# One trunk kernel: the convolution kept in fp32, VectorE making the gated products, GpSimd normalising the first token half

## The chip, the cores and the metric

The kernel runs on one core of one Trainium2 chip. The metric is the time of one execution in microseconds (us), the median of three runs.

## The reference

Two layers over 256 tokens of width 2048, all in fp32. Layer 0 mixes tokens with a gated linear recurrence, layer 1 with causal attention; each mixer is followed by a squared-ReLU MLP (2048 to 8192 and back), and each of the four sub-layers ends in `x = LayerNorm(alpha*x + sublayer(x))`. The recurrence, which the change touches:

```
gate, u = split(x @ w_in)
u = causal depthwise convolution of width 4 (u) + conv_b
r = sigmoid(u_blocks @ gate_a_w + b);  i = sigmoid(u_blocks @ gate_x_w + b)
log_a = -8 * r * softplus(-lam);       a = exp(log_a)
b = u * i * sqrt(-expm1(2*log_a))
h = associative_scan over tokens of (a, b):  h_t = a_t*h_{t-1} + b_t
y = (gelu(gate) * h) @ w_out
```

LayerNorm: mean and variance over the 2048 columns of a token, `(x-mean)*rsqrt(var+eps)*g + b`.

## The kernel before

Every large product is made of three products of fp32r operands: both factors are split into a high part (a copy rounded to fp32r) and a low part (the difference), and high*high, low*high and high*low are added in PSUM. Activations are split once; weights are split as they stream. A *turn* is 512 output columns over all 2048 inputs; its weights come in 8 *blocks* of 128x1024. For each block SyncE issues a 512 KB load into one of 8 staging buffers (`wst`, L230), ScalarE copies the high part (`split_hi`, L638), VectorE subtracts the low part (`split_lo`, L860), and TensorE multiplies. There are 4 buffers each for high and low parts, so a split may start when TensorE has finished the block four before (`mm_done`), and a load may start when the split eight before is done (`wl_done`). The order on each engine is written out by hand: `splits(b, lo, hi)` issues the splits of positions lo to hi-1 relative to the turn at block b, and the other work of the engine stands between such calls. Position 8 and above belong to the next turn's blocks. The lists `work` (L729 for ScalarE, L989 for VectorE) say after how many splits of a turn which step comes.

The recurrent mixer has four U turns (the input of the convolution), four short gate groups (L466) whose sigmoids give r (`r3`) and i (`i3`), four G turns (the gate branch), then the out projection. During the U turns the convolution of each group of 4 channel chunks is made in the scratch tile `e1` (ScalarE begins it, L662; VectorE adds three taps, L918), and its high and low parts go to `hid`, which TensorE reads for the gate groups. During the G turns GpSimd adds the two parts again into `e1`, multiplies `i3` by it (L339 to L347), and later by the root (L349 to L354); ScalarE makes the decays and roots (L704, L712), VectorE the last step of the root (L963), the scans (L969) and the product with the gate (L976). The tile `acc` (the same memory as `gate`) takes the output of the G turns, group by group (L740).

At the end of each sub-layer stands `last_pair` on TensorE (L519) and ScalarE (L746) and `last_turn` on VectorE (L1043). The last turn finishes token half 0 before half 1, so half 0's statistics are made while TensorE works on half 1. Half 0 is normalised by VectorE (column groups 0 and 1) and ScalarE (groups 2 and 3, L757), half 1 by VectorE after `add_half(1)` (L1051). TensorE then transposes the normalised tokens in eight pairs of chunks (`norm_pair`, L504), ScalarE applies gain and bias (L771), VectorE splits the result (L1071), and the next sub-layer's first turn starts. While TensorE waits it issues small dummy products (`keep_warm`, L448). The rows of gain and bias for the residual are loaded by SyncE (`load_rows`, L278) at points of its queue between the weight loads; `load_rows(2)` stands ahead of the second MLP's weights and waits for `prepped`, which VectorE raises in `prepare` (L1011).

Of the kernel before, what the change touches and what calls it, by code (L numbers as in the profile page):

```python
# [29 lines left out]
P = 128  # L30
T = 256
# [49 lines left out]
Z_DVE = 2 + NG  # L81
# [5 lines left out]
def build_trunk(nc, x, ln_g, ln_b, mlp_w1, mlp_w2, rg_w_in, rg_conv_w, rg_conv_b, rg_gate_a_w,  # L87
                rg_gate_a_b, rg_gate_x_w, rg_gate_x_b, rg_lambda, rg_w_out, moba_w_qkv, moba_w_out,
                rope, out):
    with ExitStack() as ctx:  # L90
# [27 lines left out]
        tok = sb("tok", [P, 3, HALVES])  # L118
# [22 lines left out]
        std, rstd, shift = tok[:, 0, :], tok[:, 1, :], tok[:, 2, :]  # L141
# [24 lines left out]
        ui_sum = sem("ui_sum")  # L166
# [21 lines left out]
        ln_shift = sem("ln_shift")  # L188
        z_dve = sem("z_dve")
        z_act = sem("z_act")  # L190
# [34 lines left out]
        def _(sp):  # L225
# [86 lines left out]
            load_rows(2)  # L312
# [11 lines left out]
        def _(pool):  # L324
# [13 lines left out]
            pool.wait_ge(sig_done, 4)  # L338
            for g in range(NG):  # L339
                rows = slice(g * GROUP, (g + 1) * GROUP)  # L340
                if g >= 1:
                    pool.wait_ge(ui_ready, g)
                pool.tensor_tensor(e1[:, :, :], hid[:, rows, 0, :], hid[:, rows, 1, :], ALU.add)\
                    .then_inc(ui_sum, 1)
                pool.wait_ge(ui_sum, g + 1)
                pool.tensor_tensor(i3[:, rows, :], i3[:, rows, :], e1[:, :, :], ALU.mult)\
                    .then_inc(ui_ready, 1)  # L347

            for g in range(NG):  # L349
                rows = slice(g * GROUP, (g + 1) * GROUP)  # L350
                pool.wait_ge(rec_link, g + 1)
                pool.wait_ge(ui_ready, g + 1)
                pool.tensor_tensor(i3[:, rows, :], i3[:, rows, :], r3[:, rows, :], ALU.mult)\
                    .then_inc(b_ready, 1)  # L354
# [3 lines left out]
        def _(pe):  # L358
# [145 lines left out]
            def norm_pair(n, k):  # L504

                g = 2 * k // GROUP
                pe.wait_ge(z_dve, Z_DVE * n + g + 3)
                if g >= 2:
                    pe.wait_ge(z_act, 2 * n + g - 1)
# [9 lines left out]
            def last_pair(b, ready, free, n):  # L519
# [14 lines left out]
                keep_warm(6)  # L534
# [96 lines left out]
        def _(act):  # L631
# [25 lines left out]
            def conv_hi_part(g):  # L657
                act.wait_ge(conv_link, (g + 1) * (CONV - 1))
                act.activation(hid[:, g * GROUP:(g + 1) * GROUP, 0, :], e1[:, :, :], ACT.Copy)\
                   .then_inc(conv_hi, 1)  # L660

            def conv_start(g):  # L662

                act.wait_ge(psum_free, T_U + g + 1)
                if g >= 1:
                    act.wait_ge(pair_ready, R_CONV + 2 * g)
                for c in range(g * GROUP, (g + 1) * GROUP):
                    tap = C_CONVW + (CONV - 1) * NC + c
                    ins = act.activation(e1[:, c % GROUP, :], u3[:, c, :], ACT.Identity,
# [52 lines left out]
            def product_hi(g):  # L722
# [6 lines left out]
            work = (((2, decay, 0), (2, decay, 1)), ((2, decay, 2), (2, decay, 3)),  # L729
                    ((1, root, 0), (0, root, 1), (1, root, 2), (1, root, 3), (2, gelu, 0), (0, gelu, 1)),  # L730
                    ((0, product_hi, 0), (2, product_hi, 1), (2, gelu, 2), (0, product_hi, 2)))
            for t in range(NG):
# [6 lines left out]
                splits(b, no, off, LATE)  # L739
                take_hl(t % 2, b, acc[:, t * GROUP:(t + 1) * GROUP, :], hl_copied)  # L740
# [5 lines left out]
            def last_pair(b, no, n):  # L746
# [3 lines left out]
                splits(b, no, START, BLOCKS)  # L750
                act.wait_ge(ln_var, 2 * n + 1)
                act.activation(std[:, 0:1], mv[:, 0, 1:2], ACT.Sqrt, bias=eps[:, 0:1]).then_inc(ln_root, 1)
                if n < 3:
                    splits(b, no, BLOCKS, BLOCKS + 1)
                    act.wait_ge(ln_inv, 2 * n + 1)
                    act.wait_ge(ln_shift, n + 1)
                    for g in (2, 3):  # L757
                        cols = slice(g * COLS, (g + 1) * COLS)
                        act.activation(res[:, 0, cols], res[:, 0, cols], ACT.Identity, scale=rstd[:, 0:1],
                                       bias=shift[:, 0:1]).then_inc(z_act, 1)  # L760
                        if g == 2:
                            splits(b, no, BLOCKS + 1, BLOCKS + 2)
# [92 lines left out]
        def _(dve):  # L855
# [187 lines left out]
            def last_turn(b, free, n):  # L1043
# [62 lines left out]
                for g0 in range(2):  # L1106
                    z(0, g0)
# [167 lines left out]
```

## Time and profile before

| | us |
|---|---|
| median of three runs | 2162.43 (2161.63 to 2163.31) |
| the profiled execution | 2167.35 |
| its span, first to last instruction | 2165.4 |
| TensorE busy | 2130.8 |
| VectorE busy | 1322.9 |
| ScalarE busy | 977.2 |
| GpSimd busy | 40.4 |

The page names engines PE (TensorE matmul), PEld (its weight load), DVE (VectorE), ACT (ScalarE), POOL (GpSimd) and SP (SyncE). Busy times overlap between engines. A trailing bracket in a row is the idle time of the engine ahead of it and what ended it.

### The profile page before, as it was taken

How to read it: one execution, taken by the hardware profiler on the slowest of the kernel's cores; microseconds unless marked ns; L12 is line 12 of the kernel's file. 1: busy time of each engine (PE TensorE's matmuls, PEld its weight loads, DVE VectorE, ACT ScalarE, POOL GpSimd, SP SyncE). 2: the span in 40 equal slices, each digit the busy share in tenths (PEclk: the TensorE clock that was granted, in tenths of full speed). 3: DMA queues.
4: the chain of work that ended last, by engine and by line, in shares of the span. 5: the costliest groups of instructions: out<-in, count | busy, mean ns of one | idle time of the engine just before them, and what ended most of it. 6: DMA issues, size and time to landing. Idle time of an engine off the chain costs nothing.

```text
span 2165.4 us, 31017 instructions
## 1 busy us (share of the span) xinstructions
PE 2130.8 (98%) x10966; PEld 1815.2 (84%) x10966; DVE 1322.9 (61%) x1241; ACT 977.2 (45%) x1091; POOL 40.4 (2%) x22
## 2 busy tenths in 40 slices
PE   9998999999999999999999999999999999999997
PEld 8887878888888888888888888878888888888886
DVE  6788766555554655555767566665655555555556
ACT  5585545434443443443544445344434434434442
POOL 0042000000000000000000000000000000000000
PEclk9999999999999999999999999999999999999999
DMA  8555765666666566656454546556666666566663
GB/s 275 186 167 163 243 195 175 193 195 189 187 190 192 179 198 193 185 186 194 138 177 161 185 156 218 180 189 190 194 194 186 188 192 190 175 201 186 191 190 134
DMA packets 210481, 406.14 MB, mean 188 GB/s; under 512 B 12480, under 2 KB 18880, under 8 KB 209376
## 3 DMA queue, kind: packets, MB, share of 16 engines
q1 hardware_dynamic: 210400, 405.00, 59.7%
q8 instruction: 58, 0.95, 0.2%
q14 instruction: 23, 0.19, 0.0%
HBM read 402.85 MB, written 2.10 MB: 187 GB/s over the span
## 4 chain that ended last, share of the span: by engine, by line
PE 94%; DVE 3%; issue 1%; ACT 1%; DMA 1%; SPq 0%; DVEq 0%; ACTq 0%
PE ps L383 39%; PE ps L373 32%; PE ps L374 16%; PE ps L607 1%; PE ps L605 1%; PE ps L606 1%; DVE wl L860 1%; PE ps L452 1%; PE ps L515 1%; DVE f L972 1%; ACT wh L638 0%; PE ps L620 0%; PE ps L486 0%; PE ps L487 0%; PE ps L485 0%
## 5 line engine op out<-in xcount | busy, mean ns | idle before, releaser
L860 DVE TENSOR_TENSOR wl<-wst,wh 128x1024 fp32r<-128x1024 f32 x744 | 924.1, 1251 | 666.4 <-ACT wh L638 664.4
L638 ACT ACTIVATE wh<-wst 128x1024 fp32r<-128x1024 f32 x744 | 782.9, 1059 | 905.2 <-PE ps L383 468.5
L373 PE MATMUL ps<-xin,wh 128*128 128x512 f32 x3072 | 1090.7, 400 | 7.4 <-DVE wl L860 7.4
L374 PE MATMUL ps<-xin,wl 128*128 128x256 f32 x3072 | 862.9, 281 | 0.0
L373 PEld LDWEIGHTS ps<-xin,wh 128*128 128x128 f32 x3072 | 578.4, 188 | 151.9 <-DVE wl L860 9.7
L383 PE MATMUL ps<-wh,hid 128*128 128x512 f32 x2560 | 694.9, 389 | 0.0
L374 PEld LDWEIGHTS ps<-xin,wl 128*128 128x128 f32 x3072 | 581.3, 189 | 0.2
L383 PEld LDWEIGHTS ps<-wh,hid 128*128 128x128 f32 x2560 | 479.9, 188 | 99.5
L383 PE MATMUL ps<-wl,hid 128*128 128x512 f32 x1280 | 404.4, 389 | 0.0
L383 PEld LDWEIGHTS ps<-wl,hid 128*128 128x128 f32 x1280 | 240.3, 188 | 49.9
L870 DVE TENSOR_TENSOR e<-e,ps 128x1024 f32<-128x1024 f32 x32 | 39.1, 1221 | 50.2 <-ACT e L647 50.2
L796 ACT ACTIVATE hid<-e 128x1024 f32 x32 | 34.0, 1062 | 54.6 <-DVE e L1141 54.6
L647 ACT ACTIVATE e<-ps 128x1024 f32<-128x1024 f32 x32 | 32.8, 1026 | 56.5 <-PE ps L374 56.5
L1034 DVE TENSOR_TENSOR f<-f,ps 128x1024 f32<-128x1024 f32 (+1 forms) x36 | 44.0, 1222 | 16.5 <-PE ps L383 16.5
L605 PE MATMUL ps<-wh,xin 128*128 128x512 f32 x128 | 50.7, 396 | 0.0
L607 PE MATMUL ps<-wl,xin 128*128 128x512 f32 x128 | 49.9, 390 | 0.0
L606 PE MATMUL ps<-wh,xin 128*128 128x512 f32 x128 | 49.8, 389 | 0.0
L1145 DVE TENSOR_TENSOR hid<-e,hid 128x1024 f32 x32 | 39.2, 1226 | 10.4 <-ACT hid L796 10.4
L1141 DVE SCALAR_TENSOR_TENSOR e<-e 128x1024 f32<-128x1024 f32 x32 | 39.2, 1225 | 1.1
L771 ACT ACTIVATE f<-ps,prm 128x256 f32<-128x256 f32 x48 | 24.2, 567 | 19.6 <-PE ps L515 19.6
L452 PE MATMUL ps<-ones 128*128 128x128 f32 x100 | 18.4, 350 | 12.7 <-DVE f L1051 10.5
L452 PEld LDWEIGHTS ps<-ones 128*128 128x128 f32 x100 | 16.7, 256 | 14.1 <-DVE f L1051 11.8
(116 smaller groups left out, 692.5 us busy)
## 6 DMA issues: line engine op xcount, KB each, us to landing
wst<-in_mlp_w_dram SPq DMA_DIRECT2D x512, 512.0 KB, 3.8
wst<-in_moba_w_qkv_dram SPq DMA_DIRECT2D x96, 512.0 KB, 4.1
wst<-in_rg_w_in_dram SPq DMA_DIRECT2D x64, 512.0 KB, 4.3
wst<-in_rg_w_out_dram SPq DMA_DIRECT2D x32, 512.0 KB, 3.9
wst<-in_moba_w_out_dram SPq DMA_DIRECT2D x32, 512.0 KB, 4.7
gate<-in_ln_g_dram SPq DMA_DIRECT2D x4, 1024.0 KB, 7.0
gate<-in_ln_b_dram SPq DMA_DIRECT2D x4, 1024.0 KB, 9.0
f<-in_x_dram SPq DMA_DIRECT2D x8, 256.0 KB, 7.9
```

What stands on the lines that cost most here:

```text
L373: pe.matmul(dst[:, n, :], wh[:, s, w], src[:, c, :, :], start=(c == 0), stop=False)
L374: mm = pe.matmul(dst[:, n, 0:T], wl[:, s, w], src[:, c, 0, :], start=False, stop=(c == NC - 1))
L383: return pe.matmul(banks(half)[:, a, :], hid[:, c, part, a * P:(a + 1) * P], (wl if low else wh)[:, s, w], start=(c == 0 and part + low == 0),
L452: pe.matmul(ps[:, warm_bank, 0:P], ones[:, :], ones[:, :], start=True, stop=True)
L605: pe.matmul(X[:, a, :], xin[:, c, 0, tok], wh[:, s, w], start=(c == 0), stop=False)
L606: pe.matmul(X[:, a, :], xin[:, c, 1, tok], wh[:, s, w], start=False, stop=False)
L607: mm = pe.matmul(X[:, a, :], xin[:, c, 0, tok], wl[:, s, w], start=False, stop=(c == NC - 1))
L638: act.activation(wh[:, off % SPLITS, :], wst[:, kb, :], ACT.Copy).then_inc(wh_done, 1)
L860: dve.tensor_tensor(wl[:, off % SPLITS, :], wst[:, off % BLOCKS, :], wh[:, off % SPLITS, :], ALU.subtract).then_inc(wl_done, 1)
L1034: dve.tensor_tensor(res[:, :, cols], res[:, :, cols], banks(half)[:, 0:HALVES, :], ALU.add)\
L1141: dve.scalar_tensor_tensor(out=e2[:, :, :], in0=e1[:, :, :], scalar=0.0, in1=e1[:, :, :], op0=ALU.max, op1=ALU.mult).then_inc(sq_val, 1)
L1145: dve.tensor_tensor(hid[:, rows, 1, :], e2[:, :, :], hid[:, rows, 0, :], ALU.subtract)\
```

## The change

In the mixer the convolution is accumulated in `acc` instead of `e1` and stays there in fp32 until the G turn of the same group overwrites it. GpSimd's sum of the two parts goes. The product `i3 * u` (`gated_input`) is made by VectorE in the first G turn and the product with the root by VectorE right behind the root step in the second G turn; ScalarE's roots are in the second turn instead of the third, its decays three in the first turn and one in the second. ScalarE's copy out of PSUM into `acc` waits for `ui_ready`. Scans, gelus and products have other places in the lists.

At the first three norms GpSimd normalises all of token half 0; ScalarE makes three weight copies in its place; VectorE takes the reciprocal ahead of its two splits. `keep_warm(6)` becomes `keep_warm(3)`. The third load of gain and bias rows is issued by ScalarE in the third `last_pair` instead of by SyncE.

```diff
@@ -309,7 +306,6 @@
                 load_turn(moba_w_out[0], t * COLS, B_MO + t * BLOCKS)
-            load_rows(2)
             load_mlp(1, B_MLP1)
@@ -335,23 +331,12 @@
-            pool.wait_ge(sig_done, 4)
-            for g in range(NG):
-                rows = slice(g * GROUP, (g + 1) * GROUP)
-                if g >= 1:
-                    pool.wait_ge(ui_ready, g)
-                pool.tensor_tensor(e1[:, :, :], hid[:, rows, 0, :], hid[:, rows, 1, :], ALU.add)\
-                    .then_inc(ui_sum, 1)
-                pool.wait_ge(ui_sum, g + 1)
-                pool.tensor_tensor(i3[:, rows, :], i3[:, rows, :], e1[:, :, :], ALU.mult)\
-                    .then_inc(ui_ready, 1)
-
-            for g in range(NG):
-                rows = slice(g * GROUP, (g + 1) * GROUP)
-                pool.wait_ge(rec_link, g + 1)
-                pool.wait_ge(ui_ready, g + 1)
-                pool.tensor_tensor(i3[:, rows, :], i3[:, rows, :], r3[:, rows, :], ALU.mult)\
-                    .then_inc(b_ready, 1)
+            for n in range(3):
+                for g in range(NG):
+                    cols = slice(g * COLS, (g + 1) * COLS)
+                    pool.wait_ge(ln_inv, 2 * n + 1)
+                    pool.tensor_scalar(res[:, 0, cols], res[:, 0, cols], mv[:, 0, 0:1], rstd[:, 0:1],
+                                       ALU.subtract, ALU.mult).then_inc(z_pool, 1)
@@ -504,9 +489,8 @@
                 g = 2 * k // GROUP
-                pe.wait_ge(z_dve, Z_DVE * n + g + 3)
-                if g >= 2:
-                    pe.wait_ge(z_act, 2 * n + g - 1)
+                pe.wait_ge(z_pool, NG * n + g + 1)
+                pe.wait_ge(z_dve, NG * n + g + 1)
                 if k >= 4:
@@ -531,7 +515,7 @@
                     norm_pair(n, k)
-                keep_warm(6)
+                keep_warm(3)
@@ -656,17 +640,15 @@
                 act.wait_ge(conv_link, (g + 1) * (CONV - 1))
-                act.activation(hid[:, g * GROUP:(g + 1) * GROUP, 0, :], e1[:, :, :], ACT.Copy)\
-                   .then_inc(conv_hi, 1)
+                rows = slice(g * GROUP, (g + 1) * GROUP)
+                act.activation(hid[:, rows, 0, :], acc[:, rows, :], ACT.Copy).then_inc(conv_hi, 1)
...
                 act.wait_ge(psum_free, T_U + g + 1)
-                if g >= 1:
-                    act.wait_ge(pair_ready, R_CONV + 2 * g)
                 for c in range(g * GROUP, (g + 1) * GROUP):
                     tap = C_CONVW + (CONV - 1) * NC + c
-                    ins = act.activation(e1[:, c % GROUP, :], u3[:, c, :], ACT.Identity,
+                    ins = act.activation(acc[:, c, :], u3[:, c, :], ACT.Identity,
                                          scale=prm[:, tap:tap + 1], bias=prm[:, C_CONVB + c:C_CONVB + c + 1])
@@ -726,9 +708,10 @@
-            work = (((2, decay, 0), (2, decay, 1)), ((2, decay, 2), (2, decay, 3)),
-                    ((1, root, 0), (0, root, 1), (1, root, 2), (1, root, 3), (2, gelu, 0), (0, gelu, 1)),
-                    ((0, product_hi, 0), (2, product_hi, 1), (2, gelu, 2), (0, product_hi, 2)))
+            work = (((1, decay, 0), (2, decay, 1), (2, decay, 2)),
+                    ((1, decay, 3), (2, root, 0), (0, root, 1), (1, root, 2), (1, root, 3)),
+                    ((6, gelu, 0), (0, gelu, 1)),
+                    ((1, product_hi, 0), (1, product_hi, 1), (1, gelu, 2), (1, product_hi, 2)))
             for t in range(NG):
@@ -737,6 +720,7 @@
                 splits(b, no, off, LATE)
+                act.wait_ge(ui_ready, t + 1)
                 take_hl(t % 2, b, acc[:, t * GROUP:(t + 1) * GROUP, :], hl_copied)
@@ -748,18 +732,14 @@
                 splits(b, no, START, BLOCKS)
+                if n == 2:
+                    act.wait_ge(prepped, NG * (n + 1))
+                    for dst, src in ((gain_row, ln_g), (bias_row, ln_b)):
+                        act.dma_start(dst, src[1, 0:1, :].to_broadcast([P, D])).then_inc(rows_loaded, 16)
                 act.wait_ge(ln_var, 2 * n + 1)
...
                 if n < 3:
-                    splits(b, no, BLOCKS, BLOCKS + 1)
-                    act.wait_ge(ln_inv, 2 * n + 1)
-                    act.wait_ge(ln_shift, n + 1)
-                    for g in (2, 3):
-                        cols = slice(g * COLS, (g + 1) * COLS)
-                        act.activation(res[:, 0, cols], res[:, 0, cols], ACT.Identity, scale=rstd[:, 0:1],
-                                       bias=shift[:, 0:1]).then_inc(z_act, 1)
-                        if g == 2:
-                            splits(b, no, BLOCKS + 1, BLOCKS + 2)
+                    splits(b, no, BLOCKS, BLOCKS + 3)
                 act.wait_ge(ln_var, 2 * n + 2)
@@ -772,8 +752,8 @@
                     ins.then_inc(v_done, 1)
-                    if k in (1, 2, 3, 4):
-                        off = BLOCKS + 1 + k
+                    if k in (1, 2, 3):
+                        off = BLOCKS + 2 + k
                         splits(b, no, off, off + 1)
@@ -960,11 +940,19 @@
+            def gated_input(g):
+                rows = slice(g * GROUP, (g + 1) * GROUP)
+                dve.wait_ge(sig_done, 2 * (g // 2) + 2)
+                dve.tensor_tensor(i3[:, rows, :], i3[:, rows, :], acc[:, rows, :], ALU.mult).then_inc(ui_ready, 1)
+
             def root(g):
...
                                          in1=r3[:, rows, :], op0=ALU.add, op1=ALU.mult).then_inc(rec_link, 1)
+                dve.wait_ge(ui_ready, g + 1)
+                dve.wait_ge(rec_link, g + 1)
+                dve.tensor_tensor(i3[:, rows, :], i3[:, rows, :], r3[:, rows, :], ALU.mult).then_inc(b_ready, 1)
@@ -986,10 +974,11 @@
-            work = ((), (),
-                    ((1, root, 0), (0, root, 1), (1, root, 2), (0, root, 3), (1, states, 0), (1, states, 1)),
-                    ((0, product, 0), (0, product_lo, 0), (1, states, 2), (0, product, 1), (1, product_lo, 1),
-                     (1, states, 3), (0, product, 2), (1, product_lo, 2)))
+            work = (((1, gated_input, 0), (1, gated_input, 1), (1, gated_input, 2), (1, gated_input, 3)),
+                    ((3, root, 0), (1, root, 1), (1, root, 2), (1, root, 3)),
+                    ((1, states, 0), (1, states, 1), (2, states, 2), (2, states, 3)),
+                    ((0, product, 0), (1, product_lo, 0), (0, product, 1), (1, product_lo, 1),
+                     (2, product, 2), (1, product_lo, 2)))
             for t in range(NG):
@@ -1064,8 +1053,8 @@
-                def z(h, g):
-                    dve.tensor_scalar(res[:, h, cols_for(g)], res[:, h, cols_for(g)], mv[:, h, 0:1], rstd[:, h:h + 1],
+                def z(g):
+                    dve.tensor_scalar(res[:, 1, cols_for(g)], res[:, 1, cols_for(g)], mv[:, 1, 0:1], rstd[:, 1:2],
                                       ALU.subtract, ALU.mult).then_inc(z_dve, 1)
@@ -1099,17 +1088,12 @@
                     return
-                splits(b, BLOCKS, BLOCKS + 1)
                 inverse(0)
-                dve.scalar_tensor_tensor(out=shift[:, 0:1], in0=mv[:, 0, 0:1], scalar=-1.0, in1=rstd[:, 0:1],
-                                         op0=ALU.mult, op1=ALU.mult).then_inc(ln_shift, 1)
-                for g0 in range(2):
-                    z(0, g0)
-                splits(b, BLOCKS + 1, BLOCKS + 2)
+                splits(b, BLOCKS, BLOCKS + 2)
                 add_half(1)
...
                 for g0 in range(NG):
-                    z(1, g0)
+                    z(g0)
                 for k in range(STEPS):
```

Left out: the removed semaphores and the third row of `tok`, and the convolution's lines in which `e1` becomes `acc`.

## Rows read from the trace of the kernel before

**Rows 1.** The page's busy times: engine, us, share of the span, instructions.

```profile
PE 2130.8 (98%) x10966; PEld 1815.2 (84%) x10966; DVE 1322.9 (61%) x1241; ACT 977.2 (45%) x1091; POOL 40.4 (2%) x22
```

**Rows 2.** TensorE's waits: line, releaser, us in total, times, longest us.

```profile
PE ps L452 <- DVE f L1051: 10.5, 3, 4.8
PE ps L373 <- DVE wl L860: 7.4, 7, 3.3
```

**Rows 3.** Windows: the four G turns, then four turns of an MLP; columns as printed.

```profile
core 0: us, PE busy (x) PEld busy (x) DVE busy (x) ACT busy (x) POOL busy (x), PEclk, DMA share, GB/s
126.15:226.28 100.13, 92.72 (x516) 79.12 (x515) 86.35 (x61) 64.50 (x88) 38.58 (x12) 0.98 0.51 162
502.80:593.20 90.40, 90.40 (x513) 78.37 (x513) 50.56 (x42) 39.43 (x38) 0.00 (x0) 1.00 0.61 187
```

**Rows 4.** Timeline of GpSimd in the G turns: start, us, engine, line, operation.

```profile
138.76 3.27 POOL L346 TENSOR_TENSOR f<-f,e 128x1024 f32<-128x1024 f32 x1
...
181.11 6.69 POOL L353 TENSOR_TENSOR f<-f 128x1024 f32<-128x1024 f32 x2 [25.69 <-DVE f L966]
```

**Rows 5.** Timeline of VectorE in the G turns.

```profile
130.49 26.01 DVE L860 TENSOR_TENSOR wl<-wst,wh 128x1024 fp32r<-128x1024 f32 x8 [3.40 <-ACT wh L638]
...
211.59 2.43 DVE L972 TENSOR_TENSOR_SCAN f<-f 128x256 f32<-128x256 f32 x4
```

**Rows 6.** Timeline of ScalarE in the G turns.

```profile
134.56 1.71 ACT L707 ACTIVATE f<-f,small 128x256 f32<-128x256 f32 x4
136.17 1.69 ACT L709 ACTIVATE f<-f,small 128x256 f32<-128x256 f32 x4
...
178.71 2.01 ACT L714 ACTIVATE f<-f 128x1024 f32<-128x1024 f32 x2
```

**Rows 7.** Timeline of the first norm, ScalarE, VectorE and TensorE.

```profile
309.89 0.29 ACT L752 ACTIVATE tok<-mv,eps 128x1 f32<-128x1 f32 x1 [6.07 <-DVE mv L1060]
...
310.09 1.05 ACT L638 ACTIVATE wh<-wst 128x1024 fp32r<-128x1024 f32 x1
...
311.17 1.22 DVE L860 TENSOR_TENSOR wl<-wst,wh 128x1024 fp32r<-128x1024 f32 x1 [1.31 <-ACT wh L638]
...
313.15 0.39 PE L383 MATMUL ps<-wl,hid 128*128 128x512 f32 x1
...
314.55 1.23 DVE L860 TENSOR_TENSOR wl<-wst,wh 128x1024 fp32r<-128x1024 f32 x1 [0.97 <-ACT wh L638]
...
315.69 0.68 DVE L1051 TENSOR_TENSOR f<-f,ps 128x512 f32<-128x512 f32 x1
...
316.42 2.83 PE L452 MATMUL ps<-ones 128*128 128x128 f32 x16 [2.88 <-DVE f L1051]
...
321.66 0.69 DVE L1076 TENSOR_TENSOR xin<-f,xin 128x512 fp32r<-128x512 f32 x1
...
322.07 1.50 PE L452 MATMUL ps<-ones 128*128 128x128 f32 x12
...
323.33 0.47 PE L373 MATMUL ps<-xin,wh 128*128 128x512 f32 x1
```

**Rows 8.** GpSimd's masks at L333: min/median/max ns, first and last start, forms.

```profile
L333 POOL TENSOR_SCALAR_AFFINE_SELECT maskt<-maskt x2: 295/352/408, 1.9 to 2.2; 128x128 f32<-128x128 f32 x1, 128x256 f32<-128x256 f32 x1
```

**Rows 9.** Timeline of the second norm, VectorE and TensorE.

```profile
1043.86 0.69 DVE L1076 TENSOR_TENSOR xin<-f,xin 128x512 fp32r<-128x512 f32 x1
...
1044.71 0.48 PE L373 MATMUL ps<-xin,wh 128*128 128x512 f32 x1
```

**Rows 10.** Timeline of the third norm, SyncE, ScalarE and TensorE.

```profile
1419.82 0.35 SPq L285 DMA_DIRECT2D gate<-in_ln_g_dram  x1
...
1421.32 38.12 SPq L230 DMA_DIRECT2D wst<-in_mlp_w_dram  x16
...
1428.52 1.06 ACT L638 ACTIVATE wh<-wst 128x1024 fp32r<-128x1024 f32 x1 [1.77 <-DMA wst<-in_mlp_w_dram]
...
1434.87 3.44 PE L452 MATMUL ps<-ones 128*128 128x128 f32 x16 [4.76 <-DVE f L1051]
```

More of the change, by code:

```diff
@@ L80 @@
 HELD = BLOCKS - SPLITS
-Z_DVE = 2 + NG
 C_LNG, C_LNB, C_CONVW, C_CONVB, C_BA, C_BX, C_LAM = 0, 64, 128, 192, 208, 224, 240
@@ L117, in build_trunk @@
         mv = sb("mv", [P, HALVES, 2])
-        tok = sb("tok", [P, 3, HALVES])
+        tok = sb("tok", [P, 2, HALVES])
         stat = sb("stat", [P, 4, 8])
@@ L140, in build_trunk @@
         norm_t = f3[:, :].rearrange("p (c t) -> p c t", t=T)
-        std, rstd, shift = tok[:, 0, :], tok[:, 1, :], tok[:, 2, :]
+        std, rstd = tok[:, 0, :], tok[:, 1, :]
         stage_full = [sem(f"stage_full{s}") for s in range(BLOCKS)]
@@ L165, in build_trunk @@
         sig_done = sem("sig_done")
-        ui_sum = sem("ui_sum")
         b_ready = sem("b_ready")
@@ L187, in build_trunk @@
         ln_inv = sem("ln_inv")
-        ln_shift = sem("ln_shift")
         z_dve = sem("z_dve")
-        z_act = sem("z_act")
+        z_pool = sem("z_pool")
         v_done = sem("v_done")
@@ L926, in conv_step @@
                     col = C_CONVW + (CONV - 1 - k) * NC + c
-                    ins = dve.scalar_tensor_tensor(out=e1[:, q, k:T], in0=u3[:, c, 0:T - k],
-                                                   scalar=prm[:, col:col + 1], in1=e1[:, q, k:T],
+                    ins = dve.scalar_tensor_tensor(out=acc[:, c, k:T], in0=u3[:, c, 0:T - k],
+                                                   scalar=prm[:, col:col + 1], in1=acc[:, c, k:T],
                                                    op0=ALU.mult, op1=ALU.add)
@@ L934, in conv_lo @@
                 dve.wait_ge(conv_hi, g + 1)
-                dve.tensor_tensor(hid[:, rows, 1, :], e1[:, :, :], hid[:, rows, 0, :], ALU.subtract)\
+                dve.tensor_tensor(hid[:, rows, 1, :], acc[:, rows, :], hid[:, rows, 0, :], ALU.subtract)\
                    .then_inc(pair_ready, 2)
```

## The prediction

> **What bounds the kernel now.** I read the page's busy table first: TensorE is busy 2130.8 us, 98% of the span, so only its idle stretches and its slow stretches can be won [rows 1]. The waits of TensorE say which idle stretches an engine causes: 10.5 us in three pieces behind the addition of the last sub-layer half (L1051), 7.4 us in seven pieces behind VectorE's low parts of the weights (L860) [rows 2]. Everything else of its idle time is the start and the output's tail, which the change leaves alone. Then I compared two stretches of equal work. Four turns of the gate projection take 100.13 us, four turns of the same shape inside an MLP 90.40 us with TensorE busy throughout [rows 3]. So the recurrent mixer loses 9.7 us in those four turns; the 7.4 us of waits are part of it, the rest is restarts and a granted clock of 0.98 instead of 1.00 in the same rows.
>
> Why it loses them stands in the next two groups. GpSimd runs twelve 128x1024 operations there, 3.3 us each beside VectorE [rows 4]. While it does so, eight splits of VectorE take 26.01 us, 3.25 us each [rows 5], where one alone takes 1.22 us [rows 7] (the line at 311.17). TensorE eats a block of weights in 90.40/32 = 2.83 us, so VectorE falls behind by 0.4 us a block, and by much more once the roots are added.
>
> The Trainium skill (SBUF — State Buffer, Who interferes with whom) gives the rule behind this: a VectorE instruction with two SBUF inputs and a GpSimd instruction that reads SBUF exclude one another for the whole instruction, not by halves. The trace agrees: 3.3 us is about one GpSimd operation plus one of VectorE.
>
> **Mixer, part by part.** GpSimd's twelve operations go, so VectorE's 32 splits cost 1.22 us each. VectorE gets eight new operations instead (four products u*i in the first gate turn, four with the root in the second), 128x1024 with two inputs like a split, 1.22 each, 9.8 us. Is that hidden? VectorE's work of the four turns is then 32 splits, 4 additions of the high halves, 4 root steps, 3 products and 3 low parts inside the turns and the 8 new ones, 54 x 1.22 = 65.9 us, and 16 scans at 2.43 us for four [rows 5], 9.7 us: 75.6 of 90.4 us. It fits on average; what counts is the worst place. A split may begin when TensorE ends the block four before, and is wanted three blocks later: 3 x 2.83 = 8.5 us, less the copy on ScalarE (1.05) and the split (1.22), leaves 6.2 us of debt that VectorE may run up. In the second gate turn four root pairs stand between splits: 3 x 1.22 = 3.66 us per split against 2.83, a debt of 0.83 x 4 = 3.3 us. Then come two splits and the addition, 3.66 us against 5.66, and the third turn has six splits and four groups of scans, 7.3 + 9.7 = 17.0 us against 17.0. Deepest debt about 4 us, so some 2 us remain and TensorE does not stop.
>
> ScalarE: in the first gate turn it has three decays (3.3 us each without the table load [rows 6]) between splits: 3.3 + 1.3 (load) + 1.05 = 5.7 us against 2.83, debt 2.8, paid back by the next two splits. Its eight splits, three decays, the load and the copy out of PSUM are about 20.7 of 22.6 us. In the second turn one decay, four roots of 1.0 us, a load: 18 us. The new wait ahead of the copy out of PSUM (for the product u*i of that group) has the turn's last split queued behind it; the product is ready some 10 us before, as it is VectorE's third operation. The convolution's accumulator moves to another tile with the same shapes: nothing. Its start no longer waits for the low part before it, but no TensorE wait stands in that stage: nothing. So the term is -9.7 us; bounds -10 and, if VectorE's debt overruns, -5.
>
> **Three norms.** The chain now, in the first [rows 7]: root of half 0 done at 310.18, ScalarE's split at 310.09, VectorE's at 311.17; reciprocal and two normalisations; ScalarE's next copy only at 313.5 (314.55 less its 1.05), between two normalisations; VectorE's split at 314.55; the addition of half 1 at 315.69. TensorE ended at 313.15 + 0.39 = 313.54, so this addition is 2.1 us late, which is the 2.88 us that TensorE stands. After the change ScalarE copies three blocks in a row and VectorE takes the reciprocal (0.16 us) first, then the two splits, whose copies end at 310.09 + 1.05 = 311.14 and at 312.2. Alone they would end at 313.5 and the whole 2.1 us would be won. But GpSimd starts its four 128x512 normalisations at 310.5, and two of them come in ahead of the two splits. Let p be the price of one: the addition falls at 310.5 + 2p + 2 x 1.15 + small change = 312.8 + 2p, or 313.6 if that is later; gain = 315.69 - that = 2.9 - 2p.
>
> p isn't in the trace. Nearest rows: a one-input GpSimd operation on 256 columns took 0.41 us [rows 8], the lower end; a two-input one on 1024 columns takes up to 3.4 us beside VectorE [rows 4], of which 1.2 us is VectorE's turn, so 2.2 us: the upper end, unlikely for a quarter of the operands. I take twice the first, 0.8 us, since it is one input and twice the columns. Gain 1.3 us a norm, 3.9 in all; bounds 2.1 (6.3) and -1.5 (-4.5). The addition itself has one input in PSUM.
>
> The Trainium skill (GPSIMD Engine Reference, Engine selection and its section on performance) says that a one-input operation there runs roughly at line rate and only a two-input one is held back. By that p would be near 0.5 us and the gain near 1.9 us a norm; no row here shows it.
>
> What is late next is the chain from the addition to the first product of the next turn, 315.69 to 323.33 [rows 7]. Its dummy products shrink from 12 records (322.07 to 323.33, 1.26 us) to 6: 0.63 us less. The data that the next turn waits for is there at 321.66 + 0.69 = 322.35, so all 0.63 are won. In the second norm the data comes at 1044.55 and TensorE begins at 1044.71 [rows 9]: only 0.1. The third is like the second. Together -0.8 us. GpSimd's groups 3 and 4 are wanted only inside the next turn.
>
> **Third norm.** SyncE waits there until 1419.82 to load the gain and bias rows, and only then issues the MLP's weights; the first lands so late that ScalarE stands 1.77 us, TensorE 4.76 instead of 2.88 us [rows 10]. The two row loads go to ScalarE, behind its seventh and eighth splits; the wait for the preparation is over by then (VectorE's last step is what released SyncE at 1419.82), ScalarE has nothing until the root that ends at 1428.52 - 1.77 = 1426.75, and behind the wait only the root is queued. The weights go out as buffers come free, 20 us earlier. Term: -(4.76 - 2.88) = -1.9 us.
>
> **Sum.** -9.7 - 3.9 - 0.8 - 1.9 = -16.3 us. The profiled execution took 2167.35 us (span 2165.4 plus 1.95), so it would take 2151.0. The runs shown have a median of 2162.43, 4.9 less; on them it is 2146.1. I say 2146.0.
>
> **Rivals.** (a) TensorE keeps its high clock in the norms. After 2.88 us of standing (4.76 in the third) it falls to its lower level, 1.2 of 2.4 GHz: sixteen dummy records take 2.83 us [rows 7] and 3.44 us [rows 10], against 16 x 0.105 = 1.7 us at the rate of the later twelve. Stalls of 0.3 us did not do this, 1.6 us is not in the trace. If it holds, the chain of 7 us shortens until VectorE and ScalarE carry it, by about 1.0 us a norm: 2143. For: the stand is nearly halved. Against: the dummy products are light, and the slow stretch covers them.
> (b) GpSimd is slow and the splits wait for it. p = 2.2: gain -1.5 instead of 1.3, 8.4 us more in all: 2154.5. For: the lock of rows 5. Against: one input, half the columns.
> (c) VectorE becomes the bound of the gate turns: waits for ScalarE's roots add to the debt, TensorE stands about 1 us per root or scan group, 4 to 5 us, with the clock's fall: 2151. For: 2 us of reserve are small. Against: the average of 75.6 in 90.4.
> (d) Slower than before, by one mechanism: GpSimd's normalisations ahead of the two splits, so long that they eat the mixer's gain too. The norms must then lose 9.7 + 0.8 + 1.9 = 12.4 us, 4.1 each: 2.9 - 2p = -4.1, p = 3.5 us. At p = 4 it is 2165.4. No row has anything that long for 512 columns.
> (e) The new order does not do what it says, because GpSimd's part is wanted before it is there (first group by 318.4): needs p over 2.5, so it goes with (b) and (d).
>
> **How the numbers follow.** Forecast 0.55 (2144 to 2149), (a) 0.2, (b) 0.1, (c) 0.12, (d) 0.03. The range must take in (a) with p at its lower end (2143 - 2.4 = 2140.6) and (c); most of (b) may stay out on the slow side: 2140.5 to 2153. What can be told from no change is 0.2%, 4.3 us. Faster 0.96, same 0.02 (between (b) and (d)), slower 0.02.
>
> **What would show it.** The four gate turns at 90 to 91 us with no TensorE wait on L860, and no split over 1.3 us there. The clock's dip at 0.98 of that stretch gone. In each norm TensorE standing about 1.6 us instead of 2.88, in all three alike; two splits of about 1.9 us, GpSimd's operations next to them about 0.8 us, or 2 us with the wait for VectorE. ScalarE's split of the third norm not waiting for a transfer. The forecast is wrong if the gate turns take over 93 us, if the addition of half 1 still comes 2 us after TensorE's last product, or if the dummy products run at full rate.

## The result, and the profile after

| | before | after |
|---|---|---|
| median, us | 2162.87 (4 runs) | 2142.89 (4 runs) |
| profiled execution, us | 2167.35 | 2144.91 |
| span, us | 2165.4 | 2143.1 |
| GpSimd busy, us | 40.4 | 29.8 |

The ratio is 0.9903, 95% interval 0.9891 to 0.9914: the change takes 20 us off, where 16.3 were forecast (2146.0, range 2140.5 to 2153). The time lies in the range; the mixer came out as forecast, the norms gave more than their terms. It lies outside the 2144 to 2149 that the forecast itself allowed, and on the 2143 of rival (a).

The gate turns of the profile after, beside four turns of an MLP in the same trace; this answers to [rows 3].

```profile
124.61:215.06 90.45, 90.45 (x515) 78.47 (x514) 72.10 (x70) 64.95 (x88) 0.00 (x0) 1.00 0.64 198
480.70:571.10 90.40, 90.40 (x504) 78.14 (x503) 50.54 (x42) 39.72 (x39) 0.00 (x0) 1.00 0.63 187
```

From the last gate product's start (124.48) to the out projection's first product (215.06) it is 90.6 us, 100.1 before. The mixer's turns now take what any turns of that shape take, TensorE is never idle in them and the granted clock stays at 1.00 (2.4 GHz). VectorE is less busy than before (72.1 against 86.35 us) although it does eight operations more (the window catches one split more as well). TensorE's waits answer to [rows 2]: the wait on the weights' low parts (L860 before, L840 now) is gone, and the 10.5 us behind the addition of half 1 (L1051, now L1040) are 2.3:

```profile
PE ps L437 <- DVE f L1040: 2.3, 3, 0.8
```

The first norm after the change, the timelines of ScalarE, VectorE, GpSimd and TensorE, answering to [rows 7].

```profile
298.87 2.00 ACT L622 ACTIVATE wh<-wst 128x1024 fp32r<-128x1024 f32 x2
...
298.99 0.17 DVE L1053 RECIPROCAL tok<-tok 128x1 f32<-128x1 f32 x1 [0.36 <-ACT tok L740]
300.00 2.36 DVE L840 TENSOR_TENSOR wl<-wst,wh 128x1024 fp32r<-128x1024 f32 x2 [0.84 <-ACT wh L622]
302.36 0.69 DVE L1040 TENSOR_TENSOR f<-f,ps 128x512 f32<-128x512 f32 x1
...
304.63 2.92 DVE L1057 TENSOR_SCALAR f<-f,mv,tok 128x512 f32<-128x512 f32 x4
307.47 0.41 DVE L1063 CAST xin<-f 128x512 fp32r<-128x512 f32 x1
307.92 0.69 DVE L1065 TENSOR_TENSOR xin<-f,xin 128x512 fp32r<-128x512 f32 x1
...
299.26 9.32 POOL L338 TENSOR_SCALAR f<-f,mv,tok 128x512 f32<-128x512 f32 x4 [296.69 <-DVE tok L1053]
...
301.93 0.39 PE L368 MATMUL ps<-wl,hid 128*128 128x512 f32 x1
303.10 2.41 PE L437 MATMUL ps<-ones 128*128 128x128 f32 x16 [0.78 <-DVE f L1040]
...
307.25 0.83 PE L437 MATMUL ps<-ones 128*128 128x128 f32 x6
308.71 0.47 PE L358 MATMUL ps<-xin,wh 128*128 128x512 f32 x1 [0.63 <-issue]
```

Three readings. VectorE's two splits take 1.2 us each although GpSimd works beside them throughout; the addition comes at 302.36, as soon as TensorE's last product is through (301.93 + 0.39 = 302.32). GpSimd takes 9.32 us for four operations, 2.3 us each, just above the 2.2 that was the upper end. And VectorE's four normalisations take 2.92 us, 1.92 before the change. I call the time from TensorE's last product to the first of the next turn the norm's gap. The stand is the part of it in which TensorE waits ahead of its first dummy product. The gap was 9.8, 9.4 and 11.0 us in the three norms and is 6.4, 6.3 and 6.4: 11.1 us less. The stand was 2.88, 2.88 and 4.76 us and is 0.78 in all three, and the granted clock is 1.00 in all three gaps. With 9.6 of the mixer that makes 20.7 of the 22.4 us between the two profiled executions; the other 1.7 us lie before the gate groups (last of them at 126.15 and 124.48), in a part that the change does not speed up. The first product starts at 8.10 us instead of 8.88, since the input arrived earlier in this execution, and the first products run at full rate at once, where before they took 0.63 instead of 0.40 us until about 11 us. The medians do not depend on that one start, and their difference is 20.0.

### The profile page after: what moved, and what is told of

It is laid out like the page before. It is cut to its first block, busy times and chain, and to the rows that moved or that the text cites. A ratio compares the mean times of both kernels' runs of the same rounds, so it can differ in the third digit from the quotient of the medians.

```text
span 2143.1 us, 30984 instructions
## 1 busy us (share of the span) xinstructions
PE 2122.6 (99%) x10948; PEld 1807.5 (84%) x10948; DVE 1306.1 (61%) x1240; ACT 973.7 (45%) x1085; POOL 29.8 (1%) x22
## 4 chain that ended last, share of the span: by engine, by line
PE 97%; DVE 1%; issue 1%; ACT 0%; DMA 0%; SPq 0%; DVEq 0%; ACTq 0%
PE ps L368 40%; PE ps L358 34%; PE ps L359 17%; PE ps L591 1%; PE ps L589 1%; PE ps L590 1%; PE ps L499 0%; PE ps L604 0%; PE ps L472 0%; PE ps L471 0%; PE ps L470 0%; PE ps L579 0%; DVE bnst L1047 0%; DVE f L1040 0%; DMA f<-in_x_dram 0%
## 5 line engine op out<-in xcount | busy, mean ns | idle before, releaser
L840 DVE TENSOR_TENSOR wl<-wst,wh 128x1024 fp32r<-128x1024 f32 x744 | 903.1, 1223 | 665.2 <-ACT wh L622 663.2
L338 POOL TENSOR_SCALAR f<-f,mv,tok 128x512 f32<-128x512 f32 x12 | 28.0, 2342 | 1388.2 <-DVE tok L1053 1388.2
L591 PEld LDWEIGHTS ps<-wl,xin 128*128 128x128 f32 x128 | 24.0, 188 | 5.1
```

The source lines that it names most:

```text
L591: mm = pe.matmul(X[:, a, :], xin[:, c, 0, tok], wl[:, s, w], start=False, stop=(c == NC - 1))
L840: dve.tensor_tensor(wl[:, off % SPLITS, :], wst[:, off % BLOCKS, :], wh[:, off % SPLITS, :], ALU.subtract).then_inc(wl_done, 1)
```

## The experiments

The gaps below are read as in the last paragraph, the gate turns as in the rows above. e3 to e7, e9, e11 and e12 are one execution each: from them only stretches inside the trace are read.

**One part at a time.** e1: the kernel before with the mixer's hunks alone.

> The kernel before with the mixer's part alone (convolution in fp32, products on VectorE, roots and scans at their new places); norms as before. Theory: the four gate turns fall from 100.1 to 90.4 us, the rest is unchanged, so the time falls by 9.7 us (0.45%), ratio 0.9955, and the three norms still stand 2.9, 2.9 and 4.8 us with the clock falling to 1.2 GHz in each. Rival: part of the norms' gain of the full change comes from the shifted place in time, then the chains from the addition of half 1 to the next turn's first product get shorter than 7.6, 7.3 and 7.0 us here too, and the time falls by more than 11 us.

Ratio 0.9944 (0.9927 to 0.9961), median 2152.25 against 2164.31.

```profile
126.10:216.60 90.50, 90.50 (x515) 78.46 (x514) 72.11 (x70) 64.95 (x88) 0.00 (x0) 1.00 0.64 198
...
PE ps L436 <- DVE f L1044: 10.3, 3, 4.6
```

The gate turns are those of the full change, the stands of the norms those of before. The gaps are 9.8, 9.7 and 12.4 us: not shorter, the second and third even longer than before. So no gain of the norms comes from the mixer. The time fell by 12.1 us, more than the 11 of the rival, but not for the rival's reason: the traces have 9.6 us in the gate turns, 1.6 us lost in the gaps, and 4.0 us less between the norms (711.96 to 710.52 and 385.4 to 382.9), in stretches that the edit does not touch. The forecast ratio, 0.9955, lies in the interval.

The third gap is long because the clock stayed down longer. The six us behind the stand, in e1 and then in the kernel before, columns as in [rows 3]:

```profile
1421.30:1427.30 6.00, 6.00 (x28) 6.00 (x29) 3.28 (x8) 1.62 (x4) 0.00 (x0) 0.50 0.88 323
1434.90:1440.90 6.00, 6.00 (x41) 6.00 (x42) 4.01 (x9) 2.40 (x6) 0.00 (x0) 0.76 0.89 327
```

Behind the stand this norm took 7.8 us in e1 and 6.3 before, with the same instructions. What a fallen clock costs is therefore not one number.

e2: the norms' hunks and the row loads alone.

> The kernel before with the norms' part and the moved row loads alone; GpSimd keeps its twelve products in the mixer. Theory: the mixer still takes 100.1 us for its gate turns, the norms give what they gave in the full change (3.4 + 3.1 + 4.7 = 11.1 us), ratio 0.9949; the clock stays at 2.4 GHz in the norms and falls once, in the mixer. Rival (shifted place in time): the clock falls in one or more norms although the stand is 0.8 us; each costs about 1 us, and the gain is 8 to 10 us.

Ratio 0.9944 (0.9928 to 0.9961), gate turns 100.1 us, gaps 6.4, 6.3 and 6.4, and the clock falls once, in the mixer (0.98 there, 1.00 in all three gaps). The rival falls. Its TensorE waits:

```profile
PE ps L377 <- DVE wl L859: 6.5, 8, 3.3
PE ps L456 <- DVE f L1050: 2.3, 3, 0.8
```

The product of the two ratios is 0.9888; the full change measured again (e10, below) has 0.9903 with an interval of 0.9888 to 0.9918. The times could not show a loss by overlap of under about 0.3%. In the traces the full change has the gate turns of e1 (90.6 us) and the gaps of e2, so in the stretches that were changed nothing is lost.

**The lock, and GpSimd's price.** By the lock I mean that a two-input operation of VectorE and an operation of GpSimd wait for one another. e3 adds GpSimd work on a scratch tile in the gate turns (its waits and semaphores are left out here):

```diff
+            for i in range(6):
+                pool.tensor_scalar(e1[:, 0:2, :], e1[:, 0:2, :], eps[:, 0:1], ones[:, 0:1], ALU.subtract, ALU.mult)
+            for i in range(6):
+                pool.tensor_scalar(e1[:, 0:2, :], e1[:, 0:2, :], 0.5, 1.0, ALU.subtract, ALU.mult)
+            for i in range(4):
+                pool.tensor_tensor(e1[:, 0:2, :], e1[:, 0:2, :], e2[:, 0:2, :], ALU.mult)
+            for i in range(4):
+                pool.tensor_tensor(e1[:, :, :], e1[:, :, :], e2[:, :, :], ALU.mult)
```

> The full change with GpSimd work added during the gate turns on a scratch tile, whose values nothing reads: six tensor_scalar on 128x512 with scalars from memory (the form of the norms), six with constants, four tensor_tensor on 128x512, four on 128x1024. Theory: the tensor_scalar does not lock VectorE's two-input operations out: splits beside it stay at 1.22 us, as in the norms, and it takes 2.3 us itself; beside tensor_tensor a split takes 2.2 us (512 columns) and 3.3 us (1024). Rival: every GpSimd operation that reads SBUF locks, and in the norms the splits only happened to fall between: then some splits beside tensor_scalar take 2 us and more. On the duration: if the scalars' place in memory makes it slow, constants take about 0.8 us; if the two operations a column do, constants take 2.3 us as well.

GpSimd's four kinds (min/median/max ns, first and last start), then VectorE's timeline beside them.

```profile
L342 POOL TENSOR_SCALAR e<-e,eps,ones x6: 2076/3962/4997, 130.2 to 148.0; 128x512 f32<-128x512 f32 x6
L347 POOL TENSOR_SCALAR e<-e x6: 1924/1927/2957, 152.1 to 163.0; 128x512 f32<-128x512 f32 x6
L352 POOL TENSOR_TENSOR e<-e x4: 1982/2154/2165, 166.1 to 172.6; 128x512 f32<-128x512 f32 x4
L357 POOL TENSOR_TENSOR e<-e x4: 3204/3226/3243, 174.8 to 184.8; 128x1024 f32<-128x1024 f32 x4
```

```profile
139.85 1.21 DVE L868 TENSOR_TENSOR wl<-wst,wh 128x1024 fp32r<-128x1024 f32 x1
140.99 1.63 DVE L974 TENSOR_TENSOR f<-f,gate 128x1024 f32<-128x1024 f32 x1
142.67 1.22 DVE L868 TENSOR_TENSOR wl<-wst,wh 128x1024 fp32r<-128x1024 f32 x1
143.81 1.22 DVE L974 TENSOR_TENSOR f<-f,gate 128x1024 f32<-128x1024 f32 x1
...
171.31 2.31 DVE L979 SCALAR_TENSOR_TENSOR f<-f 128x1024 f32<-128x1024 f32 x1
...
179.07 3.39 DVE L979 SCALAR_TENSOR_TENSOR f<-f 128x1024 f32<-128x1024 f32 x1
```

Beside tensor_scalar VectorE's two-input operations take 1.2 us, now and then 0.2 to 0.4 more; it is GpSimd that is stretched, up to 5.0 us. Where its operation with scalars from memory began with VectorE idle it took 2.08 us, also when a split ran beside it afterwards. Beside tensor_tensor VectorE takes 2.3 us (512 columns) and 3.4 us (1024). So who pays hangs on GpSimd's kind of operation, and the kind that was moved into the norms is the one that lets VectorE's two-input operations through. Constants instead of scalars from memory save only 0.15 us of 2.08: it is the operation, with its two steps a column, that costs about 1.9 us for 512 columns. A tensor_scalar with one step was not run, so whether the steps or the kind make it slow is open.

e4 puts the old GpSimd load back, twelve tensor_tensor of 128x1024 at the old places on a scratch tile, with VectorE's products kept:

> The full change with twelve GpSimd tensor_tensor of 128x1024 added at the old places (eight from the last sigmoid on, four behind the root steps) on a scratch tile, whose values nothing reads. Theory: the lock alone made the old mixer slow; VectorE, which now has its own products besides, falls behind by more than before: the eight splits and four products beside the first eight take 3.3 us each, TensorE stands, and the gate turns take 100 us or more instead of 90.4. Rival: what slowed the old mixer was the place of the roots and scans in the third and fourth turns; then the gate turns stay under 95 us.

The four gate turns of e4, columns as in [rows 3]:

```profile
125.60:234.80 109.20, 97.33 (x515) 82.98 (x514) 96.60 (x70) 64.81 (x88) 34.68 (x12) 0.94 0.50 159
```

109.2 us instead of 90.5. With roots and scans at their new places GpSimd's traffic brings the old loss back, and more than it, since VectorE now has its own products besides. The rival falls. Beside the first eight operations stood five splits and three products of VectorE, nearly all at 3.4 us, not the twelve of the theory. The old places of roots and scans without GpSimd's operations were not run.

In the second gate turn of e4 a product of VectorE starts right behind one of GpSimd:

```profile
173.69 2.40 POOL L345 TENSOR_TENSOR e<-e 128x1024 f32<-128x1024 f32 x1 [19.12 <-DVE f L966]
173.72 3.46 DVE L970 TENSOR_TENSOR f<-f 128x1024 f32<-128x1024 f32 x1
```

VectorE waits out the whole of GpSimd's 2.40 us. A tensor_tensor of 1024 columns took 2.38 to 2.40 us all five times that it began first (four in e4, one in the kernel before), so the 3.2 us of e3 hold its wait for VectorE: under this kind both engines pay. Per column tensor_scalar is then the slower of the two on GpSimd, 1.9 us for 512 columns against an estimated 1.2 (half of 2.40).

**The parts of the norm.** e5: the third row load back on SyncE.

> The full change with the third load of the gain and bias rows back on SyncE ahead of the second MLP's weights. Theory: only the third norm changes; ScalarE's first copy there waits for a transfer again, until about 8.7 us after VectorE's last preparation step, and the addition of half 1 comes some 3 us later; TensorE's time from its last product to the first of the next turn goes from 6.4 to about 10 us with the clock falling to 1.2 GHz; the other two stay at 6.4 and 6.3. Rival: the transfer's delay only showed because of ScalarE's normalisations before; then the third norm stays within 1 us of 6.4.

The timeline of ScalarE in the third norm of e5:

```profile
1408.49 1.06 ACT L623 ACTIVATE wh<-wst 128x1024 fp32r<-128x1024 f32 x1 [1.78 <-DMA wst<-in_mlp_w_dram]
```

The wait of 1.77 us of [rows 10] is back, and the third gap is 8.2 us instead of 6.4, the others unchanged. The load was worth 1.8 us. My expectation of 10 us was too much: the addition came 2.0 and not 3 us later (stand 0.78 to 2.74), and that stand did not bring the clock down.

e7: six dummy products behind the transposes instead of three.

> The full change with six dummy products behind the transposes as before instead of three. Theory: VectorE's low part of the first normalised columns is what the next turn waits for (0.6 us of standing behind the three), so three more cost nothing: 6.4, 6.3 and 6.4 us as with three. Rival (the forecast): fewer dummy products gave 0.6, 0.1 and 0.1 us, which come back here.

6.4, 6.3, 6.4 us: nothing comes back, and the rival falls. While the clock is up the normalised data is what the next turn waits for.

e6, e11 and e12 lengthen TensorE's stand: e6 moves VectorE's third split ahead of the addition of half 1, e11 and e12 put scratch additions there whose results nothing reads. Shown are the edit of e6 (its third split is also taken out of the later loop) and that of e11 without its waits; in e12 the second addition has 512 columns.

```diff
-                splits(b, BLOCKS, BLOCKS + 2)
+                splits(b, BLOCKS, BLOCKS + 3)
```

```diff
                 splits(b, BLOCKS, BLOCKS + 2)
+                dve.tensor_tensor(e2[:, 0:4, :], norm_t[:, 0:4, :], norm_t[:, 4:8, :], ALU.add)
+                dve.tensor_tensor(e2[:, 0:4, :], norm_t[:, 0:4, :], norm_t[:, 4:8, :], ALU.add)
```

> The full change with VectorE's third split moved ahead of the addition of half 1, so that TensorE stands 1.9 instead of 0.8 us before the first dummy products. Theory (the longer stand alone brought the clock down before): at 1.9 us it may or may not fall; if it holds, TensorE's time in a norm is 6.4 + 1.1 less what VectorE saves later, about 7.0 us; if it falls, about 8 us and more. Rival: the clock falls by where in time the stand lies, then some of the three norms show it and others do not.

> The full change with two additions of 128x1024 on a scratch tile put on VectorE ahead of the addition of half 1 in each of the three norms; nothing reads what they write. TensorE's stand ahead of the dummy products grows from 0.8 to about 3.2 us, like the 2.9 before the change. Theory (the clock's hold gave the rest of the norms' gain): it falls to 1.2 GHz in all three, and a norm takes more than 6.4 + 2.4 = 8.8 us, by the 0.5 to 1.3 us that the chain was longer before. Rival: the chain behind the addition is as short at the lower level, a norm takes 8.8 us, and that part of the gain came from something else.

> The same with one addition of 128x1024 and one of 128x512, a stand of about 2.6 us. Theory: whether the clock falls is decided by the length of the stand between 1.9 us (held in all three) and 2.9 us (fell in all three); if it holds here in all three the norms take 6.4 + 1.8 = 8.2 us. Rival: near the limit it depends on where in time the stand lies; then some of the three norms fall and others do not.

TensorE's waits of e6, e12 and e11 in that order, total and longest:

```profile
PE ps L437 <- DVE f L1040: 5.5, 3, 1.8
```

```profile
PE ps L438 <- DVE f L1043: 9.2, 3, 3.1
```

```profile
PE ps L438 <- DVE f L1043: 10.8, 3, 3.6
```

And the windows right behind the stands of e12, then of e11, columns as in [rows 3]:

```profile
305.30:310.50 5.20, 4.96 (x38) 4.37 (x38) 4.70 (x10) 2.29 (x6) 4.33 (x3) 1.00 0.12 44
1026.00:1031.20 5.20, 5.04 (x28) 4.86 (x29) 4.41 (x9) 1.62 (x4) 4.33 (x3) 0.67 0.17 61
1418.10:1423.30 5.20, 4.96 (x38) 4.37 (x38) 4.70 (x10) 2.28 (x6) 4.34 (x3) 1.00 0.13 48
```

```profile
304.80:310.00 5.20, 5.06 (x28) 4.87 (x29) 4.13 (x8) 1.59 (x4) 3.62 (x2) 0.67 0.02 8
1417.80:1423.00 5.20, 5.11 (x28) 4.92 (x29) 3.97 (x8) 1.45 (x4) 3.57 (x2) 0.67 0.01 2
```

With a stand of 1.8 us the clock holds in all three norms of e6 (gaps 7.5, 7.4, 7.5: the 1.06 us of delay and nothing else; the 0.4 us or so that I had expected VectorE to save later did not come). With 3.05 us, where I had expected 2.6, it holds in two of e12 (8.8 us) and falls in one (9.3). With 3.6 us it falls in all three of e11 (9.8, 9.8, 9.9). Before the change it fell in all three (2.88, 2.88 and 4.76 us). So near 3 us the length alone does not decide, and my length theory holds only away from there. The pattern is the one that e12's rival gives; that it is the place in time that decides is not shown, as no run changes it alone. The price is read off e12: the second norm's gap is 9.3 - 8.7 (the 0.04 us by which it is always shorter taken off) = 0.6 us longer. e11 agrees: 9.82 - 6.39 - 2.80 of added stand = 0.63. Both are prices with the new norms; the 7.8 us of e1 show that it can be more.

e9: no dummy products in the norms.

> The full change without any dummy products in the three norms. Theory: TensorE then stands about 3.5 us from its last product to the first transpose, the clock falls to 1.2 GHz in each norm as it did before the change, and the first blocks of the next turn run at that level: 6.4 us from last to first product, but 1 to 1.7 us lost behind it. Rival: the dummy products hold nothing, the clock stays up and nothing is lost.

The window of the first norm of e9, columns as in [rows 3]:

```profile
307.00:313.00 6.00, 4.55 (x23) 3.92 (x24) 5.93 (x10) 3.79 (x7) 3.80 (x2) 0.66 0.19 72
```

The clock is down during the transposes of every norm (granted 0.75, 0.65 and 0.59 there, after stands of 3.16 us). The gaps are 6.4, 6.3 and 6.6, but from the first norm's end to the second's start TensorE takes 714.2 us where the full change takes 711.9. So the dummy products hold the clock, and the theory holds for the first norm, with about 2 us. Behind the third the clock was back at once (1.00 from 1422.3 on). What the second cost can't be told: the stretch behind it, with attention in it, took 382.3 to 385.5 us over the runs, whatever they changed.

**A version from these findings.** e8 gives ScalarE the first two column groups of half 0, in its idle time between second and third copy, so that GpSimd is done before VectorE's normalisations (added lines of ScalarE only; GpSimd keeps groups 2 and 3):

```diff
+                    splits(b, no, BLOCKS, BLOCKS + 2)
+                    for g in (0, 1):
+                        cols = slice(g * COLS, (g + 1) * COLS)
+                        act.activation(res[:, 0, cols], res[:, 0, cols], ACT.Identity, scale=rstd[:, 0:1],
+                                       bias=shift[:, 0:1]).then_inc(z_act, 1)
+                    splits(b, no, BLOCKS + 2, BLOCKS + 3)
```

> The full change with the first token half's column groups 0 and 1 normalised by ScalarE, which stands idle then, between its second and third weight copy, and GpSimd keeping groups 2 and 3. Theory: GpSimd's last operation then ends before VectorE normalises half 1, whose four operations take 1.9 instead of 2.9 us, and the first product of the next turn comes 0.4 to 0.5 us earlier in each norm: 5.9 instead of 6.4 us, 1.4 us in all, below what the times can tell. Rival: VectorE is not what the chain hangs on there but ScalarE's gain and bias step; then it stays at 6.3 to 6.4 us.

> The full change again, in the same rounds as the version beside it. Theory: ratio to the kernel before 0.990 to 0.991, gate turns 90.6 us, norms 6.4, 6.3 and 6.4 us, and the parts measured alone (0.9944 and 0.9944) multiply to 0.989, within the intervals. Rival: the parts overlap and give less together than apart, then it is clearly above 0.991.

VectorE in the first norm of e8:

```profile
303.84 1.92 DVE L1069 TENSOR_SCALAR f<-f,mv,tok 128x512 f32<-128x512 f32 x4
306.25 0.43 DVE L1075 CAST xin<-f 128x512 fp32r<-128x512 f32 x1 [0.50 <-ACT f L763]
```

2.92 us are 1.92 again, and the gaps are 6.0, 5.9 and 6.0, as the theory has it. Now VectorE waits 0.5 us for ScalarE, so the rival names what is next. Ratio 0.9895 (0.9880 to 0.9909), beside it the full change (e10) 0.9903 (0.9888 to 0.9918): the traces show 1.2 us, the times can't tell them apart. e10 has the ratio, the gate turns (90.6 us) and the gaps (6.4, 6.3 and 6.4) that it was expected to have.

## Why the prediction was right, and where it fell short

- The mixer's term, -9.7 us: measured 100.1 to 90.6, so -9.6. The work of 54 operations and 16 scans on VectorE fits (72.1 us busy, 75.6 reckoned), and the reserve of about 2 us at the second gate turn was enough. e4 shows that GpSimd's operations alone, at the new places of roots and scans, bring the loss back, e1 that the term stands alone.
- The third norm's load, -1.9 us: measured 1.8 (e5). Behind the moved wait on ScalarE nothing was late.
- The order of splits and addition, -1.3 us a norm: mis-sized. Each norm got the whole 2.1 us (stand 2.88 to 0.78). The step that failed is "two of them come in ahead of the two splits", taken from the tensor_tensor rows [rows 4]: the splits did not wait. GpSimd's price was wrong too, 2.3 instead of 0.8 us; with the lock as assumed that would have been rival (b), a norm slower by 1.7 us. That two errors worked against each other is luck; what is left is a gain 2.4 us larger over the three norms. e3 shows both.
- The Trainium skill (SBUF — State Buffer, Who interferes with whom) says that a VectorE instruction with two SBUF inputs contends with a GpSimd instruction that reads SBUF, and calls the contention an exclusive lock. By that rule the splits of the norms had to wait up to 2.1 us for GpSimd; the trace does not agree for tensor_scalar (1.2 us beside a GpSimd operation of 2 to 5 us), and agrees for tensor_tensor. It also says that tensor_scalar on VectorE can take both ports and then contends: the 2.92 us against 1.92 agree.
- That 1.0 us on VectorE's normalisations of half 1 was put at nothing in the prediction. It costs 0.4 us a norm at the high clock (e8).
- The Trainium skill (GPSIMD Engine Reference, Engine selection) has one-input operations near line rate. By that p was estimated at 0.5 us; e3 has 1.93 us with constants for 512 columns, so the trace does not agree.
- The dummy products, -0.8 us: with the clock down before the change, six of them did lie on the path. Before minus after behind the stands is 1.3, 1.0 and 0.7 us, and that holds the dummy products, the clock and VectorE's longer normalisations together. Less 0.63 for the clock it leaves 0.7, 0.3 and 0.05, where 0.6, 0.1 and 0.1 stood. This is a difference and not a measurement: no run takes three of them away at the low clock. e7 shows that with the clock up they cost nothing.
- Rival (a), the clock holds, had a chance of 0.2 and came true, so by the prediction's own last sign ("if the dummy products run at full rate") the forecast was wrong on the norms. It was priced at 1.0 us a norm and is worth about 0.6 (e11, e12), an estimated 1.9 in all, more where the clock would have stayed down as long as in e1. Its price started from 1.7 us for the sixteen dummy products at full rate; at a granted clock of 1.00 they take 2.41 us, and 2.83 before. It would have come true at the 1.6 us of stand that I had expected too: at 1.8 the clock holds (e6).
- Rival (e)'s bound does not follow from its figures: with GpSimd's start at 310.5 and its first group wanted by 318.4, p would have to be 7.9 us and not 2.5. No chance and no bound of the range hung on it.

The norms together: forecast 6.6, measured 11.1. Of the 4.5 us between, 2.4 are the splits that did not wait and about 1.9 the clock. That the measured time is the 2143 of rival (a) is in part luck: it got there by both.

## What to carry to other kernels

Before an operation is moved to GpSimd, ask of which kind it is, and what VectorE does beside it: tensor_tensor held VectorE's two-input operations up, tensor_scalar did not, but four tensor_scalar of VectorE took 2.92 us beside it instead of 1.92. Here a stand of up to 2.7 us left TensorE's clock up, one of 3.6 brought it down, and around 3 us both came, so price a shorter stand with and without the clock. In a stage that one engine fills, compare it with an undisturbed stage of the same shape: the difference is the whole prize, and here it was won whole.

## What the runs showed of the hardware that I had not expected

- GpSimd's tensor_scalar on 128x512 fp32 takes 1.9 to 2.1 us alone, tensor_tensor 2.0 to 2.2 beside VectorE, its wait for VectorE included, and 2.40 on 128x1024 when it starts first; tensor_scalar beside VectorE's two-input operations up to 5.0 us, while these stay near 1.22 us.
- A stand of TensorE of 3.05 us left the clock up twice and brought it down once in one execution; 2.88 us brought it down four times out of four, twice before the change and twice in e1.
- Equal stretches far from every edit differ between executions. The four attention groups, from the first to the last start of one line of products:

```profile
L604 PE MATMUL ps<-f x32: 379/380/454, 1100.2 to 1324.8; 128*128 128x256 f32 x32
```

in the profile after, 224.6 us, and in e1, 222.0 us:

```profile
L604 PE MATMUL ps<-f x32: 379/380/454, 1107.0 to 1329.0; 128*128 128x256 f32 x32
```

That is 2.6 us with the same instructions and a granted clock of 1.00 in both. Its cause stays open; differences of this size are larger than e8's 1.2 us.
